# A decoder block: rotary halves exchanged by on-chip transfers, and one pair of expert weights held from early on

## The reference

```python
h = rms_norm(x, norm1_g)
nq, nkc, nvc, nks, nvs, nkw, nvw, ngate, fq, fk, fv, ff, gate_nsa, gate_fox = split(h @ w_in)
o_nsa = nsa_mixer(...)   # compressed + selected + window attention, 8 heads in 2 groups
o_fox = fox_mixer(...)   # causal attention with a forget gate, 8 heads
mixed = sigmoid(gate_nsa) * (o_nsa @ w_proj_nsa) + sigmoid(gate_fox) * (o_fox @ w_proj_fox)
x = x + mixed @ w_out
x = x + moe(rms_norm(x, norm2_g))   # 32 experts, 4 for each token
return rms_norm(x, norm_f_g)
```

## Time and profile before

| | us |
|---|---|
| median of 3 runs | 1562.06 |
| lowest and highest | 1559.42, 1563.93 |
| the profiled execution | 1560.53 |
| its span, first to last instruction | 1558.8 |

### The profile page before, as it was taken

One profiled execution on the slowest core, in us unless ns is written; L12 is line 12 of the kernel. 1 busy time (PEld: TensorE's weight loads), 2 busy tenths in 40 slices (PEclk: granted clock), 3 DMA queues, 4 the chain that ended last, 5 costly groups with the idle time before them and its releaser, 6 DMA issues.

```text
span 1558.8 us, 30600 instructions
## 1 busy us (share of the span) xinstructions
PE 1513.6 (97%) x12626; PEld 625.6 (40%) x12627; DVE 595.9 (38%) x1114; ACT 219.0 (14%) x468; POOL 299.5 (19%) x381
## 2 busy tenths in 40 slices
PE   7999999999999999999999999999999999999993
PEld 4654555666445433333333333333333333333331
DVE  4104555333225562244224433433343334433342
ACT  4212444323212100000000000000000000000001
POOL 2000001533000202122212221222122212121101
PEclk9999999999999999999999999999999999999997
DMA  9122130531273499999999999999999999999984
GB/s 241 28 55 54 41 81 14 167 93 27 71 290 129 172 388 403 415 417 419 414 414 419 419 413 419 417 418 412 419 419 417 411 416 418 415 418 409 412 365 135
DMA packets 109595, 463.85 MB, mean 298 GB/s; under 512 B 33698, under 2 KB 72562, under 8 KB 84464
## 3 DMA queue, kind: packets, MB, share of 16 engines
q1 hardware_dynamic: 95680, 446.42, 71.2%
q0 software_dynamic: 13872, 16.83, 4.7%
HBM read 452.94 MB, written 18.89 MB: 303 GB/s over the span
## 4 chain that ended last, share of the span: by engine, by line
PE 74%; DMA 21%; issue 2%; ACT 1%; DVE 1%; ACTq 0%; DVEq 0%; SPq 0%; PEld 0%; PEldq 0%; POOLq 0%
PE ps L1676 30%; DMA ring<-in_expert_w 20%; PE ps L1260 12%; PE ps L1685 9%; PE ps L1410 7%; PE ps L1694 4%; PE ps L1634 4%; PE ps L1395 2%; PE ps L1372 2%; PE ps L1382 2%; ACT mixT L1091 1%; PE ps L1550 0%; DMA xs<-in_x 0%; PE ps L1586 0%; DMA oT_nsa<-table,v_win 0%
## 5 line engine op out<-in xcount | busy, mean ns | idle before, releaser
L1676 PE MATMUL ps<-ring,oT_fox 128*32 128x512 f32 x6048 | 658.7, 593 | 4.5 <-DMA ring<-in_expert_w 4.0
L1676 PEld LDWEIGHTS ps<-ring,oT_fox 128*32 128x32 f32 x6048 | 194.8, 110 | 447.6 <-issue 410.4
L2332 DVE TENSOR_TENSOR mixT<-ps,mask 128x768 f32<-128x768 f32 x64 | 61.0, 953 | 577.1 <-PE ps L1676 577.1
L1685 PE MATMUL ps<-ring,hT 128*32 128x512 f32 x2048 | 267.8, 592 | 1.5 <-DMA ring<-in_expert_w 1.3
L1694 PE MATMUL ps<-ring,hT 128*32 128x256 f32 x2048 | 158.6, 379 | 0.0
L1410 PE MATMUL ps<-hT,ring 128*128 128x512 f32 x304 | 137.0, 597 | 0.0
L1694 PEld LDWEIGHTS ps<-ring,hT 128*32 128x32 f32 x2048 | 69.3, 110 | 150.0 <-issue 149.9
L910 POOL DMA_INDIRECT oT_nsa<-table,pc x93 | 105.3, 1132 | 47.1 <-POOL pc L905 27.7
L1190 ACT ACTIVATE mixT<-mixT 128x768 f32<-128x768 f32 x32 | 27.0, 844 | 614.6 <-DVE mixT L2336 614.6
L1260 PE MATMUL ps<-hT,ring 128*128 128x512 f32 x208 | 92.1, 603 | 0.2 <-ACT hT L1021 0.2
L1685 PEld LDWEIGHTS ps<-ring,hT 128*32 128x32 f32 x2048 | 68.2, 110 | 59.0 <-issue 17.8
(11 more groups left out here) (309 smaller groups left out, 1131.7 us busy)
## 6 DMA issues: line engine op xcount, KB each, us to landing
ring<-in_expert_w SPq DMA_DIRECT2D x188, 2048.0 KB, 23.3
ring<-in_w_in SPq DMA_DIRECT2D x28, 512.0 KB, 4.8
ring<-in_w_out SPq DMA_DIRECT2D x8, 512.0 KB, 9.1
ring<-in_expert_w SPq DMA_DIRECT2D x4, 1024.0 KB, 23.6
ring<-in_w_in SPq DMA_DIRECT2D x1, 2144.0 KB, 13.3
xs<-in_x SPq DMA_DIRECT2D x4, 512.0 KB, 5.1
ring<-in_w_in SPq DMA_DIRECT2D x8, 256.0 KB, 3.6
ring<-in_w_proj_nsa SPq DMA_DIRECT2D x16, 128.0 KB, 2.8
```

The costliest lines, as they stand in the source:

```text
L1676: ins = pe.matmul(wide(ps[TG * j:TG * j + TG, hc + g, :]), xT[b][:, g, c, :], up_slab(slabs[c], j), start=(c == 0), stop=(c == NK - 1), ti ...
L1685: ins = pe.matmul(ps[TG * q:TG * q + TG, bank, :], gT[b][:, q // 2, c, :], rows[:, at:at + 512], start=(c == 0 and bank == Y_BANK), stop=( ...
L2332: return dve.tensor_tensor(to, half, b_up[:, 256 * n:256 * n + 256].unsqueeze(1).broadcast_to([P, NG, 256]), ALU.add)
```

## The change

**Rotary halves.** `swap` and its six products go. SP copies the halves of 8 partitions by four transfers for each tensor, from the plain tensor into `rot`, the two tensors that later take the decay rows. GpSimd clears `rot` once. The sign goes into the frequencies of the lower halves, with two more operations on DVE. DVE waits for the four transfers and multiplies `rot` with the sines from SBUF. ScalarE waits for the first rotation before it writes q over the first plain keys. In a round, a chunk of "gf" takes the place of the product with `swap`: one chunk of "gf" stands there, two ahead of the values, and five at the end. SP issues the copies behind the q columns, and behind waits for the q before and the plain q; the last exchange stands behind the store of the decays, and the first decay rows behind the last rotation.

**The held pair.** Pair 0 of w1 of expert 17 is loaded into the whole of `xs` once the residual rows are stored and the last gather of expert 0 has landed. Expert 17 reads it there. Pair 0 of expert 18 is issued directly behind w2 of expert 16, without a wait, and the order after it is that of before. PE's loop over experts is split for this: 3 to 16, then 17, 18, a loop from 19 to 30, and 31. The last lone slab of expert 0 moves from `xs` to the second half of `mixT`, and its load from behind the second stored tile to behind the whole output projection, ahead of pair 0 of expert 1.

```diff
-PRE = ([...] + ["kc", "vc", "ks", "kw", "vs", "vw0", "vw1", "gn0", "gf0", "swks", "swkw",
-       "ffT", "gn1", "gf1", "hkv", "cq", "gn2", "gf2", "kcmp", "vcmp", "q", "gn3", "gf3", "swq"])
+PRE = ([...] + ["kc", "vc", "ks", "kw", "vs", "vw0", "vw1", "gn0", "gf0",
+       "ffT", "gn1", "gf1", "hkv", "cq", "gn2", "gf2", "kcmp", "vcmp", "q", "gn3", "gf3"])
-NSA_BODY = [("cmp", W1), ("q", W0), ("gn", W1), ("pc", W0), ("swq", W0), ("gf", W0)]
+NSA_BODY = [("cmp", W1), ("q", W0), ("gn", W1), ("pc", W0), ("gf", W0)]
...
+        rot = decay_k
...
-        FIRST_SLABS = slabs_of(W1_FIRST[0:2]) + [hT_f[:, 2 * D:4 * D], rope_pT[:, 0:2 * D], mix_f[:, 0:2 * D], xs_f[:, 0:2 * D]]
+        FIRST_SLABS = slabs_of(W1_FIRST[0:2]) + [hT_f[:, 2 * D:4 * D], rope_pT[:, 0:2 * D], mix_f[:, 0:2 * D], mix_f[:, 2 * D:4 * D]]
...
+            def swap_halves(src, to):
+                half = ROT // 2
+                for g in range(G):
+                    for k in range(2):
+                        at, other = DH * g + half * k, DH * g + half * (1 - k)
+                        sp.dma_start(rot[to][at:at + half, :], src[other:other + half, :]).then_inc(rot_loaded[to], 16)
...
+            sp.wait_ge(consts, 3)
+            for n, src in enumerate((q_plain, q_rope)):
+                sp.wait_ge(raw_k_ready, n + 1)
+                swap_halves(src, n)
...
             load_q(1)
+            sp.wait_ge(rope_done, 1)
+            sp.wait_ge(q_ready, 1)
+            swap_halves(q_plain, 0)
...
                 load_q(i + 2)
+                sp.wait_ge(rope_done, i + 3)
+                sp.wait_ge(q_ready, i + 2)
+                swap_halves(q_plain, 0)
...
+            sp.wait_ge(rope_done, PAIRS + 1)
+            sp.wait_ge(q_ready, PAIRS)
+            swap_halves(q_plain, 0)
+            sp.wait_ge(rope_done, PAIRS + 2)
             load_decay(0)
...
                     load_lone(6)
-                    sp.wait_ge(x2_stored, 16 * 2)
-                    load_lone(7)
             sp.wait_ge(out_full, 2 * NT)
+            load_lone(7)
             load_pair(1, 0)
             store_table(EARLY)
             store_x2(EARLY)
             load_pair(1, 1)
+            sp.wait_ge(x2_stored, 16 * NT)
+            sp.wait_ge(xg_loaded[0], 32)
+            src = expert_w1[0].rearrange("e (p u c) n -> e p u (c n)", p=P, c=2)
+            sp.dma_start(xs_f, src[EX, :, 0, :]).then_inc(held_loaded, 16)
             for u in range(2):
                 sp.wait_ge(w1_used, 2 * u + 2)
                 load_pair(0, NK // 2 + u)
...
-            with sp.Fori(2, E - 1) as e:
+            with sp.Fori(2, EX - 1) as e:
+                load_w1(e + 1)
+                load_w2(e)
+            load_w1(EX, 1)
+            load_w2(EX - 1)
+            load_pair(EX + 1, 0)
+            load_w1(EX + 1, 1)
+            load_w2(EX)
+            with sp.Fori(EX + 1, E - 1) as e:
                 load_w1(e + 1)
                 load_w2(e)
...
+            act.wait_ge(rope_done, 1)
             take_q(pre, "q", q_plain, SCALE)
...
-            pe.wait_ge(q_ready, 1)
-            swapped(pre, "swq", q_plain)
...
-                    pe.wait_ge(q_ready, i + 2)
-                    swapped(f, "swq", q_plain)
+                    part_gate(f, "gf", 0, 1, 0, 1)
                 turned(2 * i + 1)
...
-                    part_gate(f, "gf", 0, 1, 0, 2)
+                    part_gate(f, "gf", 0, 1, 1, 3)
...
-                    part_gate(f, "gf", 0, 1, 2, NK)
+                    part_gate(f, "gf", 0, 1, 3, NK)
...
+            for g in range(G):
+                lo = freq[DH * g:DH * g + ROT // 2, :]
+                step.link(dve.tensor_scalar(lo, lo, -1.0, None, ALU.mult))
...
-                dve.tensor_tensor(dst, work(b), rope_sin[:, :], ALU.mult).then_inc(work_free[b], 1)
-                dve.wait_ge(work_free[b], n + 1)
+            def rope(n, dst, nth=1):
+
+                dve.wait_ge(rot_loaded[n], 32 * G * nth + n + 1)
+                step.link(dve.tensor_tensor(dst, rot[n], rope_sin[:, :], ALU.mult))
```

More of the change, by code:

```diff
@@ L92 @@
 PAIRS = NH // 2
-PRE = (["hT%d" % c for c in range(NK)] + ["kc", "vc", "ks", "kw", "vs", "vw0", "vw1", "gn0", "gf0", "swks", "swkw",
-       "ffT", "gn1", "gf1", "hkv", "cq", "gn2", "gf2", "kcmp", "vcmp", "q", "gn3", "gf3", "swq"])
+PRE = (["hT%d" % c for c in range(NK)] + ["kc", "vc", "ks", "kw", "vs", "vw0", "vw1", "gn0", "gf0",
+       "ffT", "gn1", "gf1", "hkv", "cq", "gn2", "gf2", "kcmp", "vcmp", "q", "gn3", "gf3"])
 BANKS = 8
 SHARED, O_BANK, W0, W1 = 2, 5, 6, 7
-NSA_BODY = [("cmp", W1), ("q", W0), ("gn", W1), ("pc", W0), ("swq", W0), ("gf", W0)]
+NSA_BODY = [("cmp", W1), ("q", W0), ("gn", W1), ("pc", W0), ("gf", W0)]
 NSA_LAST = [("cmp", W1), ("fq", W0), ("fk", W1), ("pc", W0), ("fv", W0)]
@@ L140 @@
 N_WORK = later(N_FOX_LAST, FOX_LAST, 1)
-DVE_NSA = 27
+DVE_NSA = 28
 DVE_FOX = 9
@@ L711, in _, with load_w1 @@
                 load_pair(0, NK // 2 + u)
-            def load_w1(e):
-                for u in range(NK // 2):
+            def load_w1(e, first=0):
+                for u in range(first, NK // 2):
                     sp.wait_ge(w1_used, NK * (e - 1) + 2 * u + 2)
@@ L782, in _ @@
                                pattern=[[-1, P]], channel_multiplier=1).then_inc(consts, 1)
-            step.link(pool.memset(swap[:, :], 0.0))
-            half = ROT // 2
-            for g in range(G):
-                lo, hi = (swap[:, DH * g + half * k:DH * g + half * (k + 1)] for k in range(2))
-                step.link(pool.affine_select(out=lo, in_=lo, compare_op=ALU.not_equal, fill=-1.0,
-                                             base=-half - DH * g, pattern=[[-1, half]], channel_multiplier=1))
-                ins = pool.affine_select(out=hi, in_=hi, compare_op=ALU.not_equal, fill=1.0,
-                                         base=-DH * g, pattern=[[-1, half]], channel_multiplier=1)
-                if g:
-                    ins.then_inc(consts, 1)
-                else:
-                    step.link(ins)
+            step.link(pool.memset(rot[0], 0.0))
+            pool.memset(rot[1], 0.0).then_inc(consts, 1)
             for t in range(NT):
@@ L1307, in _ @@
             project_gates(0)
-            pe.wait_ge(consts, 3)
-            def swapped(fills, name, src):
-                w, full = bank(fills, name)
-                pe.sem_inc(pe_took, 1)
-                pe.matmul(w, swap[:, :], src, start=True, stop=True).then_inc(full, 1)
-            pe.wait_ge(raw_k_ready, 2)
-            swapped(pre, "swks", q_plain)
-            swapped(pre, "swkw", q_rope)
             w, full = bank(pre, "ffT")
@@ L1727, in down_last, with expert @@
                 used(NK // 2 - 1, ins)
-            def expert(e, b):
+            def expert(e, b, held=0):
                 if isinstance(e, int) and e == 1:
@@ L1740, in expert, with loaded @@
                 pe.wait_ge(xT_ready, e + 2)
-                up(b, slabs_of(W1_LATER),
-                   lambda c: pe.wait_ge(slabs_loaded[c // 2], 16 * e + (16 if c < LONE else 0)) if c % 2 == 0 else None, used)
+                def loaded(c):
+                    if c == 0 and held == 1:
+                        pe.wait_ge(held_loaded, 16 * PAIRS + 16)
+                    elif c == 0 and held == 2:
+                        pe.wait_ge(slabs_loaded[0], 16 * e)
+                    elif c % 2 == 0:
+                        pe.wait_ge(slabs_loaded[c // 2], 16 * e + (16 if c < LONE else 0))
+                slabs = slabs_of(W1_LATER)
+                if held == 1:
+                    slabs[0:2] = [xs_f[:, 0:2 * D], xs_f[:, 2 * D:4 * D]]
+                up(b, slabs, loaded, used)
                 second(e - 1, 1 - b)
@@ L1801, in _ @@
             expert(2, 0)
-            with pe.Fori(0, (E - 4) // 2) as i:
+            with pe.Fori(0, (EX - 3) // 2) as i:
                 expert(2 * i + 3, 1)
                 expert(2 * i + 4, 0)
-            expert(E - 1, 1)
+            expert(EX, 1, 1)
+            expert(EX + 1, 0, 2)
+            with pe.Fori(0, (E - 3 - EX) // 2) as i:
+                expert(2 * i + EX + 2, 1, 2)
+                expert(2 * i + EX + 3, 0, 2)
+            expert(E - 1, 1, 2)
             second_last(1)
@@ L1907, in _ @@
             dve.wait_ge(sines, 2)
-            rope(pre, "swks", kT_sel)
+            rope(0, kT_sel)
             rope_add(kT_sel, 1)
-            rope(pre, "swkw", kT_win)
+            rope(1, kT_win)
             rope_add(kT_win, 2)
```

14 lines of the change are left out of this document (6 added, 8 removed).

## The result

The changed kernel takes 1550.40 us in the median of five executions, the kernel before 1562.06. One of the five, of 3250.33 us, was disturbed: the other four lie between 1549.02 and 1554.28 with a median of 1549.9, and the ratio is taken without it. That ratio is 0.9931, interval 0.9916 to 0.9946: faster by 0.7%. The forecast was 1550.1. The profiled execution took 1549.43, its span is 1547.7 against 1558.8: 11.1 us less. The total agrees with the forecast; of its terms not all do, so I lay the two traces side by side from the front.

A forecast was written before the change was run, and what follows sets the result against it. TensorE was taken as the bound before the experts, the weight stream as costing 12.24 us from expert 18; 5.97 + 1.68 + 5.05 - 0.3 - 0.4 = 12.0 us off the 1562.06 median gave 1550.1, range 1546.5 to 1556.5.

The forecast's parts named there:

- Keys, 1.72: Prologue: removing the two exchange products for the keys takes 1.72 us off TensorE.
- loop, 2.58: Mixer loop: gate chunks replace the removed product, so each of three rounds is 0.86 us shorter, 2.58 us in all.
- Loop entry, 1.67: Ahead of the loop: q is done early, ScalarE's last gate evacuation is late next, and TensorE resumes 1.67 us earlier.
- The expected wait of under 1.2 us: Sign at the loop entry: TensorE's wait ahead of the loop falls under 1.2 us, from 1.80.
- Clock, 1.68: Loop entry: the shorter wait keeps TensorE's clock from falling, so the first scores take 1.68 us less.
- The rival with this term missing (1551.7): Loop entry: the clock falls all the same, 1.68 us less gain, 1551.7 us; chance 0.26.
- Cost of the transfers, 0: Rotary exchanges: the 24 transfers are hidden by other work and land with 8 us to spare in the loop; cost 0.
- The slower rival: Loop: a late exchange holds VectorE and with it TensorE; at a 16 us landing the kernel takes 1567.5 us; chance 0.03.
- Held pair, 5.05 less 0.3: Expert stage: the stream is one pair shorter from expert 17, worth 5.05 us, less 0.3 lost where the pair is loaded.
- The waits for weights from expert 23 and the lag of 7.2: Sign in the experts: TensorE waits for weights only from about expert 23; the last expert starts 7.2 us behind pace.
- A landing of 20 us: Sign in the weight stream: pairs land in near 20 us at experts 18 to 22.
- Handover, 0.4: Start of expert 1: its gathers run beside full traffic, costing 0.4 us, bounds 0 and 1.8; last table rows' gather 0.

The follow-up runs named there:

- e13_late_bank: e4_heldlate with TensorE waiting for the last gate product's bank behind its other bank waits at the loop entry; 1548.78 us, ratio 0.9919.
- e4_heldlate: Changed kernel with the eighth lone slab in its old place and the held pair issued behind the pairs of expert 0's second product; 1548.31 us, ratio 0.9925.
- e3_lone: Kernel before with only the eighth lone slab of expert 0 moved into `mixT`'s second half, loaded behind the whole output projection; 1562.46 us, ratio 1.0016.
- e2_held: Changed kernel with the `swap` products back in place of the transfers, keeping the held pair and the moved slab; 1557.09 us, ratio 0.9980.
- f1_rows: Changed kernel with each exchange cut into 32 transfers of one row in place of 4; 1588.01 us in one execution.
- e1_rot: Changed kernel without the held pair and with the eighth lone slab where it was, so the rotary part alone; 1553.78 us, ratio 0.9954.
- e5_mid: As e4_heldlate, but the held pair is issued between the weights of experts 10 and 11; 1553.52 us, ratio 0.9946.
- f2_halves: Changed kernel with each exchange cut into 8 transfers of four rows in place of 4 transfers; 1550.19 us, ratio 0.9934.

## Why the prediction held

The total held (1550.1 forecast, 1550.4 measured, 11.7 of 12.0 us), and the two mechanisms with it. Its steps, one by one:

- **Keys, 1.72, and loop, 2.58.** Right: 1.7 and 2.6. A removed product was worth its whole time, since its place was filled by products that were due anyway.
- **Loop entry, 1.67.** Mis-sized: 1.1 us. The step "what is late next is ScalarE's evacuation" was right, as `e13_late_bank` shows with 1.08 us; it left out TensorE's own instructions behind that wait, 0.43 us. The expected wait of under 1.2 us was 1.53.
- **Clock, 1.68.** Present in the two first traces and no property of the kernel: two of four executions with the 1.80 us wait fell, none of eight with 1.5. About half, not all, should have been booked; that the change prevents the fall at all is not shown by these counts. The rival with this term missing (1551.7) lies within the spread.
- **Cost of the transfers, 0.** Right. Four issues take 2.5 us, double that changes nothing, and 32 issues cost 38 us. The slower rival's mechanism exists, but its threshold lies between 8 and 32 issues.
- **Held pair, 5.05 less 0.3.** Right within what the traces can tell: 4.4 between the two profiled executions; the lag is 6.0 to 9.0 (7.6 on average) in the seven traces with the pair brought ahead of expert 1, 12.0 to 13.1 (12.5) in the four without one, which is 4.9. Its reason, "the DMA engines are busy for 17% of 536 to 544, which leaves 6.6 us", holds for the place where the pair travels, but the room is not only there: behind it, at shares of 0.9 to 1.01, the stream ran at 355 to 394 GB/s and could take 415. The waits for weights from expert 23 and the lag of 7.2 (7.86) came as forecast. A landing of 20 us could not be read off the changed kernel's trace; `e4_heldlate` has 21.3 us for an issue of 1040 to 1060, against 24.8 before.
- **Handover, 0.4.** The step that failed is "the gather of the last table rows goes out when the vector engine has its index, not when the store lands: 0". Its issue was not delayed but its data were: 4.4 us from issue to landing before, and 530.29 - 524.51, 5.8 at most, after, because the eighth slab was moved ahead of expert 1's pairs and the stores, which land later for it (`e3_lone`). The forecast had seen that later traffic, with pair 1 of expert 1 ending about 1 us later, and did not carry it over to the gather. With the fall of the clock behind that wait this is 4.2 us in the profiled execution, and 2.5 us in the medians of `e3_lone`. The gathers of expert 1, for which the forecast feared, came in time in the changed kernel: VectorE waited 0.43 us for them and TensorE not at all. There TensorE came late itself, behind the wait and the fallen clock. In `e2_held` and `f1_rows`, where the clock did not fall behind the gather of the last table rows, VectorE waits 1.04 and 2.07 us for them and TensorE 0.99 and 1.01, so the 0.4 with its bounds of 0 and 1.8 was a fair price.
- **The end, not forecast.** 1.5 us. In all ten traces with the rotary part ScalarE's table load comes 9.82 us after the operation before it, in all four without it 13.13 us; the difference is 21 turns of the skipped loop at 0.44 us in place of 0.60. Why a turn of unchanged code is longer is not settled; no run was made for it. That the shorter turn comes with the rotary part is shown by `e1_rot` and `e2_held`. Its gain is not sure: from the last expert's start to the end the four without it take 68.4 to 68.5 us, eight of the ten 66.8 to 67.7, but `e5_mid` and `f2_halves` 68.5 and 68.3. There the load of the last rows (`ring<-x`) stands in the chain with 6.67 and 6.33 us, where the changed kernel has 5.39.

So the total is right in part because errors cancelled in the profiled pair: the handover cost 3.8 us more than booked, and the start, the narrow products and the end brought 3.8 us that were not booked. The ratios to the kernel before carry the same message with less luck in them: 7.2 us for the rotary part, where 7.65 was forecast, and 3.1 for the held pair with the moved slab, where 4.35 was; both forecasts lie within the intervals.

## What to carry to other kernels

In a stream of transfers that ends up full, count the bytes that have come before it fills: a piece loaded ahead is worth its time only if it travels while GB/s is under the stream's own full rate, and the busy share is a poor guide to that (1.01 at 394 GB/s, 1.02 at 415). When a load is moved, look at what small and urgent transfer comes behind it, even 10 us later. And move data between partitions by transfers where an engine's own turn covers them: here 2.5 us of issues in a cover of 12.

## What was not expected of the hardware

- The DMA share read 1.01 with 394 GB/s in `e1_rot` and 1.02 with 415 GB/s in `e4_heldlate`, in the same stretch ahead of and behind expert 2's start.
- A loop of 21 skipped rounds took ScalarE 0.60 us a turn in the four builds with the products and 0.44 us in the ten without, with the same lines of code and the same 50 ns for its branch.
- The clock at one place in one unchanged kernel, behind one and the same wait of 1.80 us, fell to 0.50 in one profiled execution and stayed at 1.00 in another (4.11 and 2.43 us for the same 16 products).
- A transfer of 8 partitions by 2 KB within the chip's memory takes 0.62 us to issue (changed kernel), one of four rows 0.58 (`f2_halves`) and one of a single row 0.59; a single row landed in 1.7 us (median of `f1_rows`).
